# Latent attention: SyncE issues eight of each sample's sixteen page transfers, GpSimd the other eight

## What is computed

```python
PAST_LEN = 2048; PAGE_SIZE = 128          # 16 pages per sample, DEC_BATCH = 8 samples
c_past = cache_mla_latent[e][page_table].reshape(bs, past_len, KV_LORA)
k_past = cache_mla_krope[e][page_table].reshape(bs, past_len, ROPE_DIM)

def latent_scores(q_abs, q_pe, c_kv, k_pe):
    s = jnp.einsum('bqhc,bkc->bhqk', q_abs, c_kv) + jnp.einsum('bqhr,bkr->bhqk', q_pe, k_pe)
    return s.astype(jnp.float32) * MLA_SCALE

def mla_sample_attention(q_abs, q_pe, c_new, kpe_new, c_past, kpe_past):
    s_past = latent_scores(q_abs, q_pe, c_past, kpe_past)
    s_new = latent_scores(q_abs, q_pe, c_new, kpe_new)
    ...
    p = jax.nn.softmax(jnp.concatenate([s_past, s_new], axis=-1), axis=-1)
    o = jnp.einsum('bhqk,bkc->bqhc', p[..., :P].astype(c_past.dtype), c_past)
    o = o + jnp.einsum('bhqk,bkc->bqhc', p[..., P:].astype(c_new.dtype), c_new)
```

## Time and profile before

| | us |
|---|---|
| median of 3 runs | 4137.56 (4132.07 to 4141.47) |
| the profiled execution, its own time | 4124.01 |
| its span, first to last instruction | 4122.2 |
| TensorE matmuls busy | 3889.2 (94% of the span) |
| VectorE busy | 2730.5 (66%) |
| ScalarE busy | 1166.7 (28%) |
| GpSimd busy | 563.5 (14%) |

### The profile page before, as it was taken

How to read it: one execution, slowest core, us unless ns; L and a number is a source line. 1 busy time by engine, 2 the same in 40 slices (tenths; PEclk the granted TensorE clock), 3 DMA queues, 4 the chain that set the end, 5 groups by cost and what they waited for, 6 DMA issues and landing times. The chain is left out here.

```text
span 4122.2 us, 73598 instructions
## 1 busy us (share of the span) xinstructions
PE 3889.2 (94%) x26805; PEld 3645.6 (88%) x26805; DVE 2730.5 (66%) x4941; ACT 1166.7 (28%) x1569; POOL 563.5 (14%) x526
## 2 busy tenths in 40 slices
PE   8887779999999999999998977999999999999998
PEld 8763579999999998999997667999999999899997
DVE  3642247787776427888886946787777624788887
ACT  2211132233333321222213334223333322222222
POOL 0000000000000006444420000000000003544441
PEclk9988789999999999999999999999999999999999
DMA  3137423335445559999872012333544466998884
GB/s 114 46 105 251 137 79 106 110 131 166 162 164 188 174 173 245 262 259 271 261 218 76 27 51 98 110 121 132 175 166 161 166 208 184 258 268 257 270 261 128
DMA packets 301369, 694.73 MB, mean 169 GB/s; under 512 B 43809, under 2 KB 136098, under 8 KB 300834
## 3 DMA queue, kind: packets, MB, share of 16 engines
q1 hardware_dynamic: 264354, 617.19, 47.0%
q0 software_dynamic: 36864, 75.65, 7.4%
HBM read 559.39 MB, written 133.14 MB: 168 GB/s over the span
## 5 line engine op out<-in xcount | busy, mean ns | idle before, releaser
L1667 PE MATMUL ps<-peer_x_then_r_xh,experts_ul 128*128 128x260 f32 x4096 | 1164.5, 284 | 0.0
L1668 PE MATMUL ps<-experts_over_x_xl,experts_uh 128*128 128x260 f32 x4096 | 1154.5, 282 | 0.0
L1669 PE MATMUL ps<-peer_x_then_r_xh,experts_uh 128*128 128x260 f32 x4096 | 1153.2, 282 | 0.0
L1869 DVE TENSOR_TENSOR experts_ul<-experts_u,experts_uh 128x1024 fp32r<-128x1024 f32 x512 | 627.3, 1226 | 593.8 <-ACT experts_uh L1766 585.3
L1766 ACT ACTIVATE experts_uh<-experts_u 128x1024 fp32r<-128x1024 f32 x512 | 540.9, 1057 | 967.4 <-PE ps L1733 510.8
L1667 PEld LDWEIGHTS ps<-peer_x_then_r_xh,experts_ul 128*128 128x128 f32 x4096 | 771.5, 188 | 0.0
L1669 PEld LDWEIGHTS ps<-peer_x_then_r_xh,experts_uh 128*128 128x128 f32 x4096 | 769.8, 188 | 0.0
L1668 PEld LDWEIGHTS ps<-experts_over_x_xl,experts_uh 128*128 128x128 f32 x4096 | 769.6, 188 | 0.0
L1731 PE MATMUL ps<-experts_over_a_ah,experts_ul 128*128 128x448 f32 x2048 | 749.7, 366 | 11.6 <-DVE experts_over_a_al L2065 11.3
L1733 PE MATMUL ps<-experts_over_a_ah,experts_uh 128*128 128x448 f32 x2048 | 748.0, 365 | 0.0
L1732 PE MATMUL ps<-experts_over_a_al,experts_uh 128*128 128x448 f32 x2048 | 747.9, 365 | 0.0
(11 more groups left out here) (364 smaller groups left out, 4999.4 us busy)
## 6 DMA issues: line engine op xcount, KB each, us to landing
experts_u<-peer_u SPq DMA_DIRECT2D x256, 512.0 KB, 3.5
experts_u<-peer_v SPq DMA_DIRECT2D x256, 512.0 KB, 5.5
hidden<-experts_act SPq DMA_DIRECT2D x256, 260.0 KB, 2.1
gates<-experts_over_b_g SPq DMA_DIRECT2D x112, 512.0 KB, 2.9
experts_act<-hidden SPq DMA_DIRECT2D x256, 224.0 KB, 6.7
experts_over_b_g<-gates SPq DMA_DIRECT2D x64, 512.0 KB, 7.0
experts_over_b_g<-gates SPq DMA_DIRECT2D x64, 384.0 KB, 5.7
mla_ct<-cache SPq DMA_DIRECT2D x64, 320.0 KB, 4.0
```

The lines of the kernel that those rows point to most:

```text
L1667: pe.matmul(o, ul[:, b % 4, c], xh[:, c, h, 0:TH], start=(c == 0), stop=False)
L1668: pe.matmul(o, uh[:, b % 4, c], xl[:, c, h, 0:TH], start=False, stop=False)
L1669: mm = pe.matmul(o, uh[:, b % 4, c], xh[:, c, h, 0:TH], start=False, stop=(c == KC - 1))
L1869: v.tensor_tensor(ul[:, b % 4], u[:, b % 2], uh[:, b % 4].bitcast(F32), ALU.subtract).then_inc(split_done, 1)
```

## The change

`fetch_pages` gets two more arguments: the engine that issues, and `part`, the half of the sample's pages that it fetches. Its loop has two turns of four pages instead of four. SyncE fetches pages 0 to 7 of each sample with part 0, GpSimd pages 8 to 15 with part 1, for sample 0 in `latent_queries`, for samples 1 to 7 in `attention`, there behind the mask and with the same wait on `weighed`. `landed` has four semaphores: two for SyncE's halves, two for GpSimd's. The scores wait for both of a sample, each at 128 a sample instead of 256 on one.

```diff
--- before.py
+++ after.py
@@ -818,10 +818,14 @@
 
                 sp.dma_start(swapped[:], proj[ROPE:P, 3 * H + QC + CC, :]).then_inc(tables, 16)
                 sp.dma_start(a["new_lat"], ckv[:]).then_inc(stored, 16)
-                fetch_pages(sp, a, pages, ct0, 0, landed[0])
+                fetch_pages(sp, a, pages, ct0, 0, landed[0], 0)
                 sp.wait_ge(k_ready, 1)
                 sp.dma_start(a["new_kpe"], kpe[:]).then_inc(stored, 16)
                 sp.wait_ge(stored, 32)
+
+            @block.gpsimd
+            def _(pool):
+                fetch_pages(pool, a, pages, ct0, 0, landed[2], 1)
 
             @block.tensor
             def _(pe):
@@ -883,16 +887,16 @@
                     chain(v.tensor_tensor(qpe[:, h], qpe[:, h], rot[:], ALU.add))
 
 
-def fetch_pages(sp, a, pages, ct, n, landed):
-
-
-    UNR = 4
-    with sp.Fori(0, NPG // UNR) as p:
-        page = [sp.value_load(pages[0:1, bass.ds(UNR * p + (NPG * n + j), 1)], min_val=0, max_val=POOL_PAGES - 1)
+def fetch_pages(eng, a, pages, ct, n, landed, part):
+
+
+    UNR, HALF = 4, NPG // 2
+    with eng.Fori(0, HALF // UNR) as p:
+        page = [eng.value_load(pages[0:1, bass.ds(UNR * p + (NPG * n + HALF * part + j), 1)], min_val=0, max_val=POOL_PAGES - 1)
                 for j in range(UNR)]
         for j in range(UNR):
-            sp.dma_start(ct[:, bass.ds(UNR * p + j, 1)].rearrange("k o f -> k (o f)"),
-                         a["cache"][bass.ds(page[j], 1)].rearrange("o k f -> (o k) f")).then_inc(landed, 16)
+            eng.dma_start(ct[:, bass.ds(UNR * p + (HALF * part + j), 1)].rearrange("k o f -> k (o f)"),
+                          a["cache"][bass.ds(page[j], 1)].rearrange("o k f -> (o k) f")).then_inc(landed, 16)
 
 
 def attention(nc, k, a, qabs, qpe, kpe, ckv, proj, pages, ct0, landed):
@@ -989,13 +993,17 @@
                 pool.wait_ge(zeroed, 1)
                 pool.affine_select(out=mask[:], in_=mask[:], compare_op=ALU.is_ge, fill=-1.0e30, base=0,
                                    pattern=[[-1, P]], channel_multiplier=1).then_inc(masked, 1)
+                for n in range(1, TS):
+                    if n >= 2:
+                        pool.wait_ge(weighed, n - 1)
+                    fetch_pages(pool, a, pages, ct[n % 2], n, landed[2 + n % 2], 1)
 
             @block.sync
             def _(sp):
                 for n in range(1, TS):
                     if n >= 2:
                         sp.wait_ge(weighed, n - 1)
-                    fetch_pages(sp, a, pages, ct[n % 2], n, landed[n % 2])
+                    fetch_pages(sp, a, pages, ct[n % 2], n, landed[n % 2], 0)
 
             @block.tensor
             def _(pe):
@@ -1012,7 +1020,8 @@
                     mm.then_inc(s_ready, 1)
 
                 def sample_scores(n):
-                    pe.wait_ge(landed[n % 2], 16 * NPG * (n // 2 + 1))
+                    pe.wait_ge(landed[n % 2], 8 * NPG * (n // 2 + 1))
+                    pe.wait_ge(landed[2 + n % 2], 8 * NPG * (n // 2 + 1))
                     if n:
                         pe.wait_ge(sexped, n)
                     for c in range(CC + 1):
@@ -1278,7 +1287,7 @@
             qpe = t.sb("qpe", [ROPE, H, T])
             pages = t.sb("pages", [1, TS * NPG], I32)
             ct0 = t.sb("ct0", [P, NPG, 2 * KVL + PAGE])
-            landed = [t.sem(f"landed{b}") for b in range(2)]
+            landed = [t.sem(f"landed{b}") for b in range(4)]
             with Stage(nc, "uq") as u:
                 wuq = u.sb("wuq", [P, QC, 2 * H * P])
                 wuk = u.sb("wuk", [P, H, KVL])
```

## The result

Six runs of the changed kernel have a median of 4110.86 us (4101.77 to 4119.63), six of the kernel before 4130.14 us (4125.6 to 4141.47). The ratio is 0.9949, 95% interval [0.9932, 0.9967]. A second, later set of the same kernel has a median of 4106.97 us and a ratio of 0.9926 [0.9904, 0.9949]. The change saves 0.5 to 0.7%, by these ratios 21 and 31 us, by the medians 19 and 27; forecast were 23 us and a time of 4114.5 us. That time was counted from 4137.56 us, the median of the first three runs of the kernel before; six runs have 4130.14.

The account below looks back on a forecast made before the run. SyncE's reading and issuing, 20.8 us a sample, was taken as the bound. With GpSimd sharing, (20.7 + 14) / 2 gives a 17.35 us beat and sample 7 starts 23 us earlier: 4137.56 - 23 = 4114.5 us, range 4100 to 4138.

Parts of the forecast that it names:

- GpSimd's price: Attention stage, GpSimd's issuing: 1.38 us a transfer, taken from its gathers, plus 2.9 us of reading per group of four.
- what is late next is GpSimd's half: After the change the score matmuls L1021 would still be what waits, now on the pages GpSimd fetches.
- The landing: Time from a page transfer's issue to its arrival: 5 us taken, against a 3.9 us median from SyncE.
- F: Attention stage: time from a buffer's release until the sample fetched into it is complete, 20.7 us.
- TensorE's own time: P, TensorE's work on one sample in the attention stage without waiting: 13.6 to 14.9 us, taken as 14.
- two-buffer rule: Sample n's pages are asked for once n-2 is weighed, so two samples take F + P: beat 17.35 us.
- no change: Rival: the 16 DMA engines limit the page transfers whoever issues; 4138 us, chance 0.05.
- Two queues moving less: Rival: with both issuers the engines are full at 258 GB/s, 20.3 us a sample; gain 7 us, 4130; chance 0.13.
- The slow GpSimd: Rival: GpSimd issues above a 1.89 us pitch and the kernel slows, at 2.3 us to 4160; chance 0.13.
- The fast rival: Rival: GpSimd's reads overlap its transfers and the moving limits; beat 16.7 us, gain 30 us, 4108; chance 0.17.
- The lock of GpSimd's port by VectorE: VectorE's probability scalings may stall GpSimd's transfers: at most 6 us lost in all, left out of the sum.
- far end of 1.99 us: GpSimd's pitch per transfer if its price goes by rows, 128 against a gather's 72; 5 us lost in all.

Follow-up runs that it names:

- the one taken apart above: Sample 2's fetch in the changed kernel with each issuer also waiting until its half of the sample before landed, reads after that wait: stage 142.7 us, ratio 0.9960.

## Why the prediction was right

The bound was named rightly, and three runs show it. SyncE's cycle of reading and issuing was the beat: take the reads away and the beat falls to 16.9 us on the same queue; make a read 0.15 us cheaper and it falls to 18.3, the length of SyncE's round; give the whole to GpSimd, whose group costs 5.4 us instead of 5.2, and it rises to 22.1. The total came out at 21 and 31 us saved, for 23. That it came so near is in part luck, as the sizes show.

The steps, one by one:

- SyncE's eight issues take 7.2 us, as forecast.
- GpSimd's price was twice too high. Forecast were 1.38 us a transfer by its gathers and 12 to 14 us for its eight; measured are 0.65, and 342.80 - 334.89 = 7.9 us. It is done with a sample 11.3 us after the release, not 17.1. So GpSimd never set the beat, and "what is late next is GpSimd's half" did not hold as stated: SyncE, equally done in 10.1 us, sees its pages land as late.
- The moving was under-rated: 322 to 349 GB/s forecast as the full rate, 385 to 414 measured. The bursts of before lasted under 3 us and never showed the engines at their best. At 397 GB/s 5.24 MB take 13.2 us. So the sixteen pages are sent in 8.4 us (334.42 to 342.80) and moved in 13, and the last ones wait for those ahead of them.
- The landing was therefore under-rated: 5 us forecast, 7.2 measured in the median, and for the last pages of sample 2 9.1 (GpSimd's, 342.27 to TensorE's start at 351.37) and 10.1 (SyncE's).
- These errors cancel, which is luck and no merit of the sum: F was forecast as 15.7 us to the last issue and 5 to its landing, 20.7 us, and came out for sample 2 as 10.8 and 9.1, 19.9 us; for samples 4 and 6 it is 20.5.
- TensorE's own time, 14 us, is in truth 12.6 for an odd sample and 14.1, 17.1, 17.1 for samples 2, 4 and 6. There the clock is low after the wait: 0.67 in the first 4.6 us for sample 2, 0.50 from 385.96 to 391.00 for sample 4. Two samples take 34.6 and 37.6 us; forecast 34.7.
- The waits were forecast as 2 to 6 us each for every sample; they are 7.4 to 8.1 for every second one. The two-buffer rule was right, but it asks for one wait in two samples, and I spread it. Sample 2 is asked for at 331.52 and wanted 12.4 us later, before its 19.9 us are over. Sample 3 is asked for at 343.93 and wanted at 365.29, 21.4 us later, when it is there. In my working GpSimd's 17.1 us kept it back.
- The saving up to sample 7's start, measured from sample 0: 143.65 - 122.48 = 21.2 us, forecast 22.9. A term was missing: sample 7 then runs at full clock, 4.9 us more. Together 26.1.
- The DMA share over the stage was forecast near 0.9 and is 0.73, where it was 0.70: it is 0.91 from sample 2's first issue to the release of its buffer (334.42 to 365.46), but the engines stand still before each even fetch and after the last one.
- The query stage costs nothing, as forecast: from its first load to attention's first matmul 43.5 us before (262.99 to 306.48) and 43.65 after (268.04 to 311.69).

Of the 26.1 us the profiled spans show 15.4. The stage began 5.2 us later, and the part behind it took 5 us longer (from the first matmul of `latent_values` to the end 3636.4 us before, 3641.5 after). Both are scatter: in the ten profiled executions, with the same code there, the query stage begins between 262.9 and 269.4, and the part behind takes from 3636 to 3652 us. It is why totals here need several runs.

Of the rivals, no change is refuted by both sets. Two queues moving less is refuted by the 385 to 414 GB/s. The slow GpSimd is refuted by 536 ns. The fast rival came true in half: the moving and not GpSimd sets what is left, but GpSimd's reads do not overlap its transfers, 2.93 us lie between two groups. Its time can't be told from the forecast's by the totals: it said 4108, the forecast 4114.5, the two sets have 4110.86 and 4106.97. The beat of 18.2 us is nearer to the forecast's 17.35 than to its 16.7, and slower than both. What the sum had no term for is the start and end of a fetch, 1.4 and 2.2 us in the one taken apart above; the landing time stood in for them. The rule of the Trainium skill (DMA: Bandwidth & Descriptors, Issuing engines are not separate DMA queues), that several issuers save the sequencer's time alone, agrees with these runs: one queue reaches the same 395 GB/s. Only "usually small" fails here, with 20.8 us of reading and issuing against 13.2 of moving.

The lock of GpSimd's port by VectorE, which the Trainium skill names (SBUF — State Buffer, Who interferes with whom), is to be seen, and it is cheap. In the stage only two of GpSimd's 56 issues last longer than 559 ns, and they are the two that lie beside a scaling of VectorE (L1130, 0.68 us for its two instructions, here from 320.96 and from 376.90): 731 ns for the one at 320.8 and this one:

```profile
L898 POOL DMA_DIRECT2D mla_ct<-cache x1: 676/676/676, 376.8 to 376.8; - x1
```

The changed kernel's second execution has 731 and 676 ns at the same two places. That is 0.2 and 0.1 us over the 536 of the others, where the prediction allowed 6 us in all; the other scalings fall where GpSimd issues nothing.

## What to carry to other kernels

Where transfers have addresses out of registers, lay the reads and the issues of one cycle end to end on the issuing engine: if they are longer than the moving, the issuer is the bound, although SyncE never shows as busy. A second issuer helps then, and so do cheaper reads (written out, with constant addresses of the table entries, and ahead of the wait); both together gave the shortest stage, 117.6 us against 158.0. When the DMA engines are filled by bursts of a few transfers, the rate in the bursts need not be their limit: here it was 349 GB/s, and 385 to 418 with more in flight. And where TensorE waits at intervals, count the clock beside the wait: of the 26.1 us saved in the stage, 9.2 were matmuls that ran faster.

## What was not expected of the hardware

A plain transfer of 128 rows of 2560 bytes costs GpSimd 536 ns (a pitch of 0.65 us), about half of a gather of 72 rows (0.95 us at least). So the rows alone do not set the price, as the prediction's far end of 1.99 us had it; which difference between the two kinds of transfer does was not tried. And a fetch that was alone in the engines needed 1.4 us before data flowed and 2.2 us from the last of them to TensorE's start; with a second fetch in flight the engines stay full meanwhile.
